# First modulation summed and used in two halves of the features, and the first norm's squares added by GpSimd

## What is computed

```python
mod = jax.nn.silu(c) @ w_ada[l] + b_ada[l]
shift1, scale1, gate1, shift2, scale2, gate2 = [m[:, None, :] for m in jnp.split(mod, 6, axis=-1)]

h = rms_norm(x, norm1_w[l]) * (1.0 + scale1) + shift1
proj = h @ w_in[l]
```

## Time and profile before

| | |
|---|---|
| median of 3 runs | 1661.54 us (1660.48 to 1663.36) |
| profiled execution, its own time | 1661.04 us |
| its span, first to last instruction | 1659.2 us |
| PE busy | 96% |
| DVE, ACT, POOL busy | 60%, 46%, 49% |
| from the span's start to the first product's matmul | 47.70 us |

### The profile page before, as it was taken

How to read it: one execution, slowest core, us unless ns; L and a number is a source line. 1 busy time by engine, 2 the same in 40 slices (tenths; PEclk the granted TensorE clock), 3 DMA queues, 4 the chain that set the end, 5 groups by cost and what they waited for, 6 DMA issues and landing times. The chain is left out here.

```text
span 1659.2 us, 23401 instructions
## 1 busy us (share of the span) xinstructions
PE 1591.4 (96%) x8072; PEld 1315.4 (79%) x8072; DVE 1002.9 (60%) x1321; ACT 755.8 (46%) x1376; POOL 814.1 (49%) x578
## 2 busy tenths in 40 slices
PE   4899999999999899999999999999999999999997
PEld 4678888888878688888878888888888778777776
DVE  4788888888739688487342221212278865657562
ACT  2476667656633544323243232323467645433332
POOL 1266576766756510156644444444644556333424
PEclk9999999999999999999999999999999999999999
DMA  7243343444332200277523333333332333211202
GB/s 302 67 133 111 120 135 109 120 134 127 109 94 62 74 12 16 71 245 253 180 59 107 91 100 97 99 97 95 96 89 84 90 107 102 71 51 52 64 20 89
DMA packets 76245, 171.28 MB, mean 103 GB/s; under 512 B 8241, under 2 KB 8625, under 8 KB 72817
## 3 DMA queue, kind: packets, MB, share of 16 engines
q1 hardware_dynamic: 68832, 133.09, 27.2%
q10 hardware_dynamic: 7312, 36.83, 6.2%
HBM read 167.67 MB, written 2.23 MB: 102 GB/s over the span
## 5 line engine op out<-in xcount | busy, mean ns | idle before, releaser
L576 POOL TENSOR_TENSOR w_lo<-w_raw,w_hi 128x512 fp32r<-128x512 f32 x457 | 683.8, 1517 | 611.0 <-ACT w_hi L620 610.4
L1083 PE MATMUL bank<-a_hi,w_hi 128*128 128x512 f32 x1040 | 416.4, 400 | 12.4 <-DVE a_lo L1621 7.3
L1085 PE MATMUL bank<-a_hi,w_lo 128*128 128x512 f32 x1040 | 407.2, 392 | 0.0
L1084 PE MATMUL bank<-a_lo,w_hi 128*128 128x512 f32 x1040 | 407.0, 391 | 0.0
L620 ACT ACTIVATE w_hi<-w_raw 128x512 fp32r<-128x512 f32 x457 | 263.2, 620 | 159.7 <-PE bank L1085 127.8
L1083 PEld LDWEIGHTS bank<-a_hi,w_hi 128*128 128x128 f32 x1040 | 196.6, 189 | 59.7 <-issue 10.6
L1083 PE MATMUL bank<-b_hi,w_hi 128*128 128x512 f32 x600 | 235.7, 393 | 2.0 <-DVE gate_silu L2073 2.0
L1085 PE MATMUL bank<-b_hi,w_lo 128*128 128x512 f32 x600 | 233.7, 390 | 0.0
L1084 PE MATMUL bank<-b_lo,w_hi 128*128 128x512 f32 x600 | 233.6, 389 | 0.0
L1085 PEld LDWEIGHTS bank<-a_hi,w_lo 128*128 128x128 f32 x1040 | 196.6, 189 | 42.3
L1084 PEld LDWEIGHTS bank<-a_lo,w_hi 128*128 128x128 f32 x1040 | 196.9, 189 | 41.6 <-issue 1.9
(11 more groups left out here) (329 smaller groups left out, 2488.1 us busy)
## 6 DMA issues: line engine op xcount, KB each, us to landing
w_raw<-ws SPq DMA_DIRECT2D x457, 256.0 KB, 2.7
cs_rows<-cs_scratch ACTq DMA_DIRECT2D x16, 1024.0 KB, 5.1
ada_piece<-ada ACTq DMA_DIRECT2D x16, 1024.0 KB, 5.7
ada_piece<-ada SPq DMA_DIRECT2D x8, 1024.0 KB, 14.9
x_stream<-x SPq DMA_DIRECT2D x1, 2048.0 KB, 16.4
x_stream<-x ACTq DMA_DIRECT2D x1, 2048.0 KB, 8.2
out<-x_stream SPq DMA_DIRECT2D x8, 256.0 KB, 2.1
rope_table<-rope ACTq DMA_DIRECT2D x1, 512.0 KB, 4.0
```

What stands on the lines that cost most here:

```text
L576: nc.gpsimd.tensor_tensor(wlo[b][:, :], raw[n % RAW_RING][:, :], r32(whi[b][:, :]), ALU.subtract)\
L1083: mm(out, lh, rh, start=first, stop=False)
L1084: mm(out, lh, rl, start=False, stop=False)
L1085: return mm(out, ll, rh, start=False, stop=last)
```

## The change

Two things are done.

1. `POOLED` gets an entry for the first norm, `"n1": KT - 1`. POOL now adds the squares of tiles 0 to 6 (6 additions), PE sums that total and the square of tile 7 (8 matmuls of one column instead of 32). ACT's reuse of a buffer `sq` waits for POOL's additions instead of PE's sums. POOL makes these additions before its first `low`.
2. The last of the 8 pieces of `w_ada` is added in two halves of 2 x 512 columns (`ada_add_last`): the shift and scale of features 0 to 511, then those of 512 to 1023. PE sums each half with 8 matmuls of its own. DVE forms the first half of `gain1`, starts `norm_split`, and forms the second half inside it, ahead of tile 4 (`first_modulation`).

```diff
-POOLED = {"ssd": PAIRS - 1, "n2": KT - 2, "na": KT - 1, "nkv": KT - 1, "fin": KT - 2}
+POOLED = {"n1": KT - 1, "ssd": PAIRS - 1, "n2": KT - 2, "na": KT - 1, "nkv": KT - 1, "fin": KT - 2}
...
+def half_columns(half):
+    return [part * KT + k for part in range(2) for k in range(half * KT // 2, (half + 1) * KT // 2)]
...
+            squares[0] = [("n1", m) for m in range(1, POOLED["n1"])]
...
             for k in range(KT):
                 stat("n1", k)
-            rows("n1")
-            ada_reduce(acc, 0)
+            for half in range(2):
+                if half:
+                    rows("n1")
+                    pe.wait_ge(ada_acc, KT)
+                else:
+                    pe.wait_ge(half_added, 1)
+                for b in half_columns(half):
+                    ins = mm((ADA, STF)[half][:, b:b + 1], acc[:, b * P:(b + 1) * P], ones[:, 0:1], start=True, stop=True)
+                ins.then_inc(ada_red if half else half_reduced, 1)
...
+            def ada_add_last(half):
+                p, w = KT - 1, slice(half * D_MODEL // 2, (half + 1) * D_MODEL // 2)
+                if half == 0:
+                    ve.wait_ge(ada_in[p % ADA_RING], 16 * (p // ADA_RING + 1))
+                    ve.wait_ge(ada_acc, p)
+                into, src = (b[:, :].rearrange("p (s w) -> p s w", s=2)[:, :, w] for b in (acc, piece[p % ADA_RING]))
+                V.scalar_tensor_tensor(into, src, csl[:, p:p + 1], into, ALU.mult, ALU.add)\
+                    .then_inc(ada_acc if half else half_added, 1)
...
+            def first_modulation(half):
+                k0, k1 = half * KT // 2, (half + 1) * KT // 2
+                ve.wait_ge(ada_red if half else half_reduced, 1)
+                out, summed, bias = (b.rearrange("p (s k) -> p s k", s=2)[:, :, k0:k1] for b in (
+                    modc[:, 0:2 * KT], (ADA, STF)[half][:, 0:2 * KT], col("bada", 0, 2 * KT)))
+                V.tensor_tensor(out, summed, bias, ALU.add).then_inc(mod_ready if half else half_mod, 1)
+                ve.wait_ge(mod_ready if half else half_mod, 1)
+                v(V.scalar_tensor_tensor(gain1[:, k0:k1], modc[:, KT + k0:KT + k1], 1.0, col("norm1", k0, k1 - k0), ALU.add, ALU.mult))
+                v.settle()
...
+                    if k == KT // 2 and second_half:
+                        second_half()
...
-            inverse("n1")
-            ada_add(KT - 1, acc)
-            ada_finish(0)
-            v(V.scalar_tensor_tensor(gain1, modc[:, KT:2 * KT], 1.0, col("norm1", 0, KT), ALU.add, ALU.mult))
-            v.settle()
-            wait_rows("n1")
+            ada_add_last(0)
+            inverse("n1")
+            ada_add_last(1)
+            first_modulation(0)
+            wait_rows("n1")
```

More of the change, by code:

```diff
@@ L401, in build @@
         ada_acc, ada_red, mod_ready = sem("ada_added"), sem("ada_reduced"), sem("mod_ready")
+        half_added, half_reduced, half_mod = sem("ada_half_added"), sem("ada_half_reduced"), sem("mod_half_ready")
         c_th = sem("silu_c")
@@ L1612, in wait_rows, with norm_split @@
                 ve.wait_ge(rows_ready, ROOT_AT[norm] + 1)
-            def norm_split(n0, gain, hi, lo, hi_sem, hi0, rdy, shift=None):
+            def norm_split(n0, gain, hi, lo, hi_sem, hi0, rdy, shift=None, second_half=None):
                 def low(k):
@@ L1642, in _ @@
                 ada_add(p, acc)
+            ada_add_last(0)
             inverse("n1")
-            ada_add(KT - 1, acc)
-            ada_finish(0)
-            v(V.scalar_tensor_tensor(gain1, modc[:, KT:2 * KT], 1.0, col("norm1", 0, KT), ALU.add, ALU.mult))
-            v.settle()
+            ada_add_last(1)
+            first_modulation(0)
             wait_rows("n1")
-            norm_split(0, lambda k: gain1[:, k:k + 1], aH, aL, hiA, 0, rdyA, lambda k: modc[:, k:k + 1])
+            norm_split(0, lambda k: gain1[:, k:k + 1], aH, aL, hiA, 0, rdyA, lambda k: modc[:, k:k + 1],
+                       lambda: first_modulation(1))
             def log1p(e, z, z2, p):
```

## The result

The changed kernel takes 1665.18 us (median of 16 runs), the kernel before 1659.63 us (16 runs). The ratio is 1.0032, with a 95% interval from 1.0022 to 1.0042: 3.7 to 7.0 us slower. The forecast was 6.0 us slower. As a time it was 1667.6 us, 2.4 above the measured one: 1.9 of that is the kernel before, whose median is 1659.63 here and was 1661.54 when the forecast was made, and 0.5 is the sum itself. The profiled execution took 1666.3 us, 5.3 over the one of before.

What follows compares the result with a forecast made beforehand. PE is busy 96% of the span, so opening delays pass to the end; they hang on the root and POOL's first low part. 5.20 + 0.41 + 0.43 = 6.04 us over 1661.54 gives 1667.6, range 1663.8 to 1669.8.

Steps and rivals of the forecast that it cites:

- its main case: POOL and DVE take turns and the whole shift reaches the end: chance 0.76, between 1665.5 and 1669 us.
- The turns: In the opening, POOL's additions of squares and DVE's pieces alternate, 3.29 us a turn; PE's sums end 7.09 us later.
- POOL's first low part: Behind the root, held 1.07 us less by DVE's shorter second half; ends at 44.89, 6.02 us later.
- The first `a_hi`: On ACT behind slabs 4 to 6, from 46.04 to 51.24: +5.20 us (6.02 - 0.82).
- The collision: DVE's first `a_lo` must wait for POOL's seventh low part: +0.41 us.
- The second modulation: The second half's forming stands in DVE's queue ahead of tile 4's `t`: +0.43 us.
- the rival: Engines behind PE's idle time return perhaps half of 6 us: 1664.5; with some additions slipping, chance 0.08, 1663 to 1665.
- the additions run beside DVE's pieces: POOL's additions take 1.31 us each, not slowed by DVE: -2.4 us, 1659.1; chance 0.10, 1658 to 1661.
- DVE gets in ahead of POOL: DVE's next piece precedes a waiting POOL, whose additions 2 to 6 come after: 1.9 us later, 1669.5; chance 0.06.
- The gain of the halves: DVE has both `t` at 48.2, 3 us ahead of ACT, so the earlier modulation's gain stays hidden.

Runs made afterwards that it cites:

- the halves alone: Changed kernel without the squares on POOL, so the kernel before plus only the modulation in halves; ratio to the kernel before 0.9989.
- the slabs moved: Kernel before plus the modulation in halves, with ACT rounding slabs 4 to 6 behind all eight `a_hi`; run twice, 0.9984 and 0.9973 of the kernel before.
- the sum in PSUM: Changed kernel with DVE's running sum of the modulation in four PSUM banks until the last piece; ratio to the kernel before 0.9983.
- the slabs late: Changed kernel with ACT rounding slabs 4, 5 and 6 behind the 4th, 6th and 8th `a_hi`; ratio to the kernel before 1.0024.
- the slabs last: Kernel before with only ACT's rounding of slabs 4 to 6 moved behind all eight `a_hi`; ratio to the kernel before 1.0014.

## Why the prediction was right, step by step

The forecast was right in its mechanism: each step below came as described, and the sizes differ by little. The measured 1665.18 us lies just under the 1665.5 to 1669 of its main case, because the kernel before was 1.9 us faster in these runs than in the three at hand then.

**The turns.** Held: 3.29 us a turn was read from the earlier trace rows, 3.27 measured; the additions 2 to 6 end where they were put, within 0.1 us once `x`, which landed 0.31 us earlier in this execution, is taken into account. The root was forecast 7.09 us later and came 6.80 later, 7.11 relative to `x`. (The forecast wrote 8 x 0.43 as 3.42; 8 times 13.78 / 32 is 3.44, which changes nothing.) The Trainium skill (SBUF — State Buffer, its two separate sides) gives a blocked instruction's resumption as about 115 ns after the other's end, measured there on a DMA whose descriptors GpSimd writes. By an estimate from that figure POOL would have ended 1.38 us after DVE; it ended 1.13 after it here too, less than the 1.26 of an addition alone, and the measurement decides. The page's rule is that a DVE instruction with two SBUF inputs and a GpSimd one that reads SBUF exclude each other. The trace agrees: 14.75 us for five additions with DVE's sum in SBUF, 6.90 with it in PSUM.

**POOL's first low part.** Forecast +6.02, measured 38.87 to 44.59, +5.72 (6.03 relative to `x`). The shorter second half gave back the 1.07 us as forecast.

**The first `a_hi`.** Forecast +5.20, measured +4.68 (4.99 relative to `x`). The remaining 0.2 is that ACT starts `a_hi` 0.09 us before the end of the slab's instruction in the record, and that the loads came slightly sooner. This is the term that was furthest off, by 0.2 us relative to `x`, and it is the size, not the mechanism.

**The collision.** Forecast +0.41, measured +0.49 (1.24 against 0.75).

**The second modulation.** Forecast +0.43, measured 0.40 (55.63 to 56.03).

Together 4.66 for the first `a_lo`'s start, 0.49 and 0.40 make 5.55, and `dt` is evacuated 5.55 us later, the mixer's first square 5.5 later, the median of the timed runs 5.55 higher. That the median agrees to the hundredth is luck, with an interval of 3.7 to 7.0 us. Relative to `x` the shift of `dt` is 5.86 us, so the forecast of 6.04 is even nearer. Nothing was given back up to the mixer's first square, and half of it given back in the end lies outside the interval: the rival is out as it was priced, though a microsecond or two would not show. Out too is the one in which the additions run beside DVE's pieces, and the one in which DVE gets in ahead of POOL, since every turn in the trace is POOL's after DVE's.

**The gain of the halves** was said to be hidden behind ACT; the halves alone (0.9 us) and with the slabs moved (4.8 to 5.4 us at `dt`) show that.

**The price of the first rival** (additions beside DVE's pieces, 2.4 us faster than before) can be read as well: with the sum in PSUM, where they do run beside them, `dt` came 2.6 us earlier than before. DVE's instructions are others there, so that the two agree to 0.2 us is partly luck. The forecast had chosen between the two cases by the earlier trace rows.

## What to carry to other kernels

Before work is moved to GpSimd to relieve TensorE, look at what VectorE does in the same microseconds: if it runs long instructions with both inputs in SBUF, each GpSimd instruction waits for one of them and holds up the next (here an addition came every 3.27 us instead of taking 1.26, and a piece took 3.14 us instead of 2.35). Take the price of a turn from a place where the trace already shows the two side by side, and put one of VectorE's operands in PSUM if both must run. And before a result is made earlier, ask what else the consumer's engine has written in its program ahead of it: here three slabs on ACT hid 4 of the 5 us that the halves are worth at `dt`.

## What the runs showed of the hardware that I had not expected

How much small VectorE instructions suffer: 128x4 in 1.20 us instead of 0.16 and 128x256 in 1.18 instead of 0.42, when a low part of POOL is under way. In the runs here moving the slabs did not remove this, it only chose which instruction was hit: the first `a_lo` in the changed kernel, three of them with the slabs late, `dt_work` with the slabs last.
